# A norm and rotation phase in another order: head statistics, rotations and gate pieces of two attentions

## What is computed

```python
def mla_mixer(c_q, c_kv, k_rope, g_qa, w_uq, g_kva, w_ukv, g_qn, g_kn, cos, sin):
    q = (rmsnorm(c_q, g_qa) @ w_uq).reshape(b, s, 4, 96)
    kv = (rmsnorm(c_kv, g_kva) @ w_ukv).reshape(b, s, 4, 128)
    k_nope, v = split(kv, [64])                 # k = [k_nope, k_rope]
    q = rmsnorm(q, g_qn); k = rmsnorm(k, g_kn)  # over the 96 of a head
    q, k = rotated in their last 32 of 96
    return softmax(q k^T / sqrt(96)) v          # 4 heads

def diff_mixer(q_in, k_in, v_in, g_qn, g_kn, ..., g_sub):
    q = apply_rope(rmsnorm(q_in.reshape(b, s, 8, 32), g_qn))
    k = apply_rope(rmsnorm(k_in.reshape(b, s, 8, 32), g_kn))
    o = (softmax(q1 k1^T) - lam * softmax(q2 k2^T)) v      # 4 heads
    return rmsnorm(o, g_sub) * (1 - lambda_init)

merged = sum over the branches n (mla, fnet, diff, hgrn) of
         sigmoid(gate_logits_n) * (o_n @ w_branch[n])
x = x + merged @ w_out; then a feed-forward part
```

## Time and profile before

| | us |
|---|---|
| median of three runs | 3875.69 (3874.26 to 3875.77) |
| the profiled execution | 3875.1 |
| its span, first to last instruction | 3873.0 |
| PE busy | 3719.0 (96%) |
| VectorE busy | 1826.0 (47%) |
| ScalarE busy | 1360.0 (35%) |
| GpSimd busy | 255.7 (7%) |
| mean granted clock of TensorE | 0.983 of full |

### The profile page before, as it was taken

One profiled execution on the slowest core, in us unless ns is written; L12 is line 12 of the kernel. 1 busy time (PEld: TensorE's weight loads), 2 busy tenths in 40 slices (PEclk: granted clock), 3 DMA queues, 4 the chain that ended last, 5 costly groups with the idle time before them and its releaser, 6 DMA issues.

```text
span 3873.0 us, 44934 instructions
## 1 busy us (share of the span) xinstructions
PE 3719.0 (96%) x16592; PEld 2902.9 (75%) x16592; DVE 1826.0 (47%) x2405; ACT 1360.0 (35%) x2102; POOL 255.7 (7%) x154
## 2 busy tenths in 40 slices
PE   6999699999999999999999999999999999999999
PEld 5888478887887777888756677878875666787887
DVE  7743677424333555333354657443333555654332
ACT  3222332223323554232343434332234344433321
POOL 2000200000000000000010101200000010120000
PEclk8999899999999999999999999999999999999999
DMA  7843268433332221333312122333341122232332
GB/s 268 266 135 95 84 213 268 146 100 88 97 96 85 60 64 58 102 94 95 114 47 56 50 69 58 93 92 94 95 118 49 49 59 61 63 90 88 97 94 86
DMA packets 639945, 390.83 MB, mean 101 GB/s; under 512 B 17856, under 2 KB 601408, under 8 KB 638656
## 3 DMA queue, kind: packets, MB, share of 16 engines
q1 hardware_dynamic: 634432, 376.82, 32.9%
q10 hardware_dynamic: 5376, 12.14, 0.9%
HBM read 386.81 MB, written 2.10 MB: 100 GB/s over the span
## 4 chain that ended last, share of the span: by engine, by line
PE 90%; DVE 5%; issue 2%; ACT 1%; POOL 1%; DMA 0%; ACTq 0%; DVEq 0%; POOLq 0%
PE bank L1969 25%; PE bank L1971 24%; PE bank L1970 24%; PE bank L2150 2%; PE bank L2109 1%; PE bank L1984 1%; PE bank L1985 1%; PE bank L1986 1%; PE bank L2142 1%; PE bank L2252 1%; POOL ssum L716 1%; PE bank L2294 1%; PE bank L1995 1%; PE bank L2090 1%; PE bank L2133 1%
## 5 line engine op out<-in xcount | busy, mean ns | idle before, releaser
L1296 DVE TENSOR_TENSOR w_lo<-stage,w_hi 128x1024 fp32r<-128x1024 f32 x564 | 695.7, 1234 | 1432.9 <-ACT w_hi L779 1432.3
L1969 PE MATMUL bank<-h_hi,w_hi 128*128 128x512 f32 x3008 | 1199.9, 399 | 36.9 <-DVE h_lo L1543 27.0
L1971 PE MATMUL bank<-h_hi,w_lo 128*128 128x512 f32 x3008 | 1175.6, 391 | 0.0
L1970 PE MATMUL bank<-h_lo,w_hi 128*128 128x512 f32 x3008 | 1175.4, 391 | 0.0
L779 ACT ACTIVATE w_hi<-stage 128x1024 fp32r<-128x1024 f32 x564 | 596.7, 1058 | 1224.9 <-PE bank L1971 1212.9
L1969 PEld LDWEIGHTS bank<-h_hi,w_hi 128*128 128x128 f32 x3008 | 568.0, 189 | 176.5 <-DVE h_lo L1543 29.4
L1970 PEld LDWEIGHTS bank<-h_lo,w_hi 128*128 128x128 f32 x3008 | 568.0, 189 | 122.2 <-issue 8.0
L1971 PEld LDWEIGHTS bank<-h_hi,w_lo 128*128 128x128 f32 x3008 | 567.1, 189 | 120.3
L1971 PE MATMUL bank<-a_hi,w_lo 128*128 128x512 f32 x1056 | 410.9, 389 | 0.0
L1969 PE MATMUL bank<-a_hi,w_hi 128*128 128x512 f32 x1056 | 410.9, 389 | 0.0
L1970 PE MATMUL bank<-a_lo,w_hi 128*128 128x512 f32 x1056 | 410.9, 389 | 0.0
(11 more groups left out here) (259 smaller groups left out, 3693.9 us busy)
## 6 DMA issues: line engine op xcount, KB each, us to landing
stage<-in_ffn_w_in SPq DMA_DIRECT2D x176, 512.0 KB, 3.8
stage<-in_w_in SPq DMA_DIRECT2D x108, 512.0 KB, 3.8
stage<-in_w_gate_up SPq DMA_DIRECT2D x88, 512.0 KB, 3.7
ada_stage<-in_ada_w SPq DMA_DIRECT2D x128, 256.0 KB, 3.9
work<-in_ada_w SPq DMA_DIRECT2D x128, 256.0 KB, 5.5
stage<-in_ffn_w_out SPq DMA_DIRECT2D x64, 512.0 KB, 3.5
stage<-in_w_down SPq DMA_DIRECT2D x32, 512.0 KB, 3.7
stage<-in_ffn_w_out SPq DMA_DIRECT2D x32, 384.0 KB, 3.1
```

The lines of the kernel that those rows point to most:

```text
L1296: nc.vector.tensor_tensor(lo, stage[:, slot * WORDS:(slot + 1) * WORDS], hi.bitcast(F32), ALU.subtract).then_inc(w_lo_ready, 1)
L1969: nc.tensor.matmul(dst, wh, chunk(hi, k), start=first and a == 0, stop=False)
L1970: nc.tensor.matmul(dst, wh, chunk(lo, k), start=False, stop=False)
L1971: ins = nc.tensor.matmul(dst, wl, chunk(hi, k), start=False, stop=last and a == len(ks) - 1)
```

## The change

Nothing is computed otherwise; instructions of every engine's list change places.

- MLA: PE lays the statistics in pairs: two, a quarter of gate 1, two, the value parts, two, a quarter of gate 1, two, the other half of gate 1. VectorE squares the query heads when the query parts are out and normalises four while the others are under way; ScalarE makes the roots in two groups around the value copies.
- MLA, rotations: PE does rotations 0 to 3, branch 1, gate 2, rotations 4 to 7, branch 2, fill 3. VectorE does its part of fill 1 behind the first four rotations, of fill 2 behind the other four.
- Diff: the roots of the two query chunks stand on ScalarE ahead of the sixth projection's copy. VectorE rotates all four chunks ahead of fill 8; PE does gate 8, rotations, branch 8, fills 9 and 10.
- GpSimd does the diff cosines ahead of merge 8, not behind it.
- Diff's attention with `tail=True`: gate 15 is laid into the last head (three of eight steps ahead of its transposes, five behind), and branch 15 behind it; the first hgrn projection follows, then the statistics of the result.

The diff, with the surroundings cut (in the order of the file: GpSimd, ScalarE, VectorE, PE):

```diff
...
             cosines(mla_ropes)
-            merge(step[1], DIFF_FILL)
             pool.wait_ge(rope_loaded, 32 * (step[1] + 1))
             cosines(diff_ropes)
-            for f in range(DIFF_FILL + 1, MERGES):
+            for f in range(DIFF_FILL, MERGES):
                 merge(step[1], f)
...
 
-    def attention(at_, fills):
+    def attention(at_, fills, tail=False):
         heads = at_["heads"]
...
                 output_high(h)
-            if not last:
+            if not last or tail:
                 fill(fills + h + 1)
...
         parts([wk(MLA_K + h)[0:64] for h in range(4)])
+        roots(mla_head_norms(l)[0:4])
         parts([token_rows(MLA_V, t) for t in range(TB)])
-        roots(mla_head_norms(l))
+        roots(mla_head_norms(l)[4:8])
         fill(MLA_FILL + 1)
...
         n.zbase = n.z
-        for c in range(6):
+        for c in range(5):
             project("diff", c, wk(c))
+        roots(diff_norms(l)[0:2])
+        project("diff", 5, wk(5))
         branch_high(DIFF_FILL)
         parts([token_rows(DIFF_V, t) for t in range(TB)])
-        roots(diff_norms(l))
+        roots(diff_norms(l)[2:4])
         fill(DIFF_FILL)
-        split_roped(diff_ropes, 0, 3)
+        split_roped(diff_ropes, 0, 4)
         fill(DIFF_FILL + 1)
-        split_roped(diff_ropes, 3, 4)
         fill(DIFF_FILL + 2)
-        attention(diff_attention(), DIFF_FILL + 3)
+        attention(diff_attention(), DIFF_FILL + 3, tail=True)
         roots(diff_sub_norms)
-        fill(DIFF_FILL + 7)
+
+        n.zbase = n.z
+        project("hgrn", H_ORDER[0], wk(H_ORDER[0]), func=ACT.Sigmoid)
         act.wait_ge(gnormed, n.item)
         splits([wk(DIFF_O + c) for c in range(2)], 2)
-
-        n.zbase = n.z
-        for c in H_ORDER[:6]:
+        for c in H_ORDER[1:6]:
             project("hgrn", c, wk(c), func=ACT.Sigmoid)
...
 
-    def attention(at_, fills):
+    def attention(at_, fills, tail=False):
         heads = at_["heads"]
...
         output_low(len(heads) - 1)
+        if tail:
+            fill(fills + len(heads))
         n.block += TB * mp * len(heads)
...
         fill(MLA_FILL)
+        heads = mla_head_norms(l)
+        dve.wait_ge(z_ready, n.z + 4)
+        squares(heads[0:4])
+        dve.wait_ge(z_ready, n.z + 8)
+        dve.wait_ge(kr_placed, l + 1)
+        squares(heads[4:6])
+        normalise(heads[0:4])
+        squares(heads[6:8])
+        normalise(heads[4:8])
         n.z += 12
-        dve.wait_ge(z_ready, n.z - TB)
-        dve.wait_ge(kr_placed, l + 1)
-        heads = mla_head_norms(l)
-        squares(heads)
-        normalise(heads)
-        fill(MLA_FILL + 1)
         dve.wait_ge(gnormed, n.item)
...
         ropes(mla_ropes, 0, 4)
+        fill(MLA_FILL + 1)
+        ropes(mla_ropes, 4, 8)
         fill(MLA_FILL + 2)
-        ropes(mla_ropes, 4, 8)
         fill(MLA_FILL + 3)
...
         normalise(norms)
-        fill(DIFF_FILL)
         dve.wait_ge(gnormed, n.item)
         dve.wait_ge(rope_loaded, 32 * (l + 1))
-        ropes(diff_ropes, 0, 3)
+        ropes(diff_ropes, 0, 4)
+        fill(DIFF_FILL)
         fill(DIFF_FILL + 1)
-        ropes(diff_ropes, 3, 4)
         fill(DIFF_FILL + 2)
-        attention(diff_attention(), DIFF_FILL + 3)
+        attention(diff_attention(), DIFF_FILL + 3, tail=True)
         dve.wait_ge(o_ready, n.opair)
...
         normalise(diff_sub_norms)
-        fill(DIFF_FILL + 7)
+        next_weights("hgrn", H_ORDER[0])
         splits([wk(DIFF_O + c) for c in range(2)], 2)
 
-        for c in H_ORDER[:4]:
+        for c in H_ORDER[1:4]:
             next_weights("hgrn", c)
...
 
-    def attention(at_, l, fills):
+    def attention(at_, l, fills, tail=False):
 
...
             last = h + 1 == len(heads)
+            filled = not last or tail
             if not last:
                 scores(h + 1, first)
-                if cut:
-                    gate(fills + h + 1, 0, cut)
+            if filled and cut:
+                gate(fills + h + 1, 0, cut)
             pe.wait_ge(p_scaled, (n.head + h + 1) * TB)
...
             turn(h, 1)
+            if filled:
+                gate(fills + h + 1, cut, DC)
             if not last:
-                gate(fills + h + 1, cut, DC)
                 scores(h + 1, middle)
...
             weigh(h, TB - 1)
-            if not last:
+            if filled:
                 branch(l, fills + h + 1)
...
                                             stop=True))
+        heads = mla_head_norms(l)
+        stats(heads[0:2])
+        gate(MLA_FILL + 1, 0, 2)
+        stats(heads[2:4])
         w_v = w_ukv.rearrange("p (h c) -> p h c", h=4)[:, :, 64:P]
...
                                             stop=True))
-        stats(mla_head_norms(l))
-        fill(l, MLA_FILL + 1)
+        stats(heads[4:6])
+        gate(MLA_FILL + 1, 2, 4)
+        stats(heads[6:8])
+        gate(MLA_FILL + 1, 4, DC)
         pe.wait_ge(z_ready, n.z)
+        pe.wait_ge(gnormed, n.item - 4)
+        ropes(mla_ropes, 0, 4)
+        branch(l, MLA_FILL + 1)
+        gate(MLA_FILL + 2)
         pe.wait_ge(gnormed, n.item)
-        ropes(mla_ropes, 0, 4)
-        fill(l, MLA_FILL + 2)
         ropes(mla_ropes, 4, 8)
+        branch(l, MLA_FILL + 2)
         fill(l, MLA_FILL + 3)
...
         stats(norms[2:4])
-        fill(l, DIFF_FILL)
+        gate(DIFF_FILL)
         pe.wait_ge(z_ready, n.z)
...
         ropes(diff_ropes, 0, 4)
+        branch(l, DIFF_FILL)
         fill(l, DIFF_FILL + 1)
...
         pe.wait_ge(qk_ready, n.qk)
-        attention(diff_attention(), l, DIFF_FILL + 3)
-        gate(DIFF_FILL + 7, 0, 4)
+        attention(diff_attention(), l, DIFF_FILL + 3, tail=True)
+
+        n.zbase = n.z
+        project("hgrn", H_ORDER[0])
         stats(diff_sub_norms)
-        gate(DIFF_FILL + 7, 4, DC)
-        branch(l, DIFF_FILL + 7)
-
-        n.zbase = n.z
-        for c in H_ORDER:
+        for c in H_ORDER[1:]:
             project("hgrn", c)
...
```

## The result

The changed kernel takes **3850.4 us** (median of four runs, 3848.2 to 3853.4), the kernel before 3875.7 (3874.3 to 3877.6): ratio 0.9934, interval 0.9920 to 0.9949. It is faster by 25.3 us, where 21.7 were forecast; 3854.0 (3844 to 3868) was the prediction.

The account below looks back on a forecast made before the run. PE bounds the kernel, losing time to idling and low clock in three stretches per layer. MLA 13.4, diff 0.5 and last head 7.3 sum to 21.2 off 3875.1: 3853.9, the median 0.6 above, so 3854 (3844 to 3868).

Parts of the forecast that it names:

- MLA, statistics: MLA's statistics, spread between gate quarters and value parts, cost PE zero idle, so it reaches the rotations at 2002.2.
- MLA, rotations: With fills behind each four rotations on VectorE, MLA's scores start 5.2 us earlier in one layer, 3.9 in layer 1.
- The rival with fills in the quiet: GpSimd's later cosines leave fill 1 and the last low halves alone: 8 us faster, 3846; chance 0.13.
- The scores' clock: MLA's first scores run at the high clock level after a short last wait: 2.3 us more, 2.0 in layer 1.
- Diff, rotations: In differential attention, a new 5.5 us wait at branch 9 replaces waits of 3.34 and 2.0: 0.5 us gained in all.
- Last head: At diff's last head, gate 15 matmuls fill idle before the transposes and statistics follow the first hgrn projection: 7.3 us.
- The rule on ACT_TABLE_LOAD: A ScalarE table switch costs a 1.38 us drain besides its load, delaying the third projection: gain 2.8 us less.
- The slower rival: GpSimd's cosines hold VectorE for all their time in the MLA and diff chains: 3880; chance 0.05.

Follow-up runs that it names:

- diff_fill_inside: The changed kernel with VectorE's fill 8 in the differential attention between its first two and last two rotations, ScalarE's splits divided to match: 3839.2 us.
- mla_only: The kernel before with only the MLA part of the change (statistics, fills, root groups): 3860.2 us.
- mla_early_ropes: The changed kernel with PE's first four MLA rotations ahead of gate 1's last piece, and ScalarE's first query split ahead of gate 1's tanh: 3862.5 us.
- diff_norm_only: The kernel before with only the differential attention's norm and rotation changed (roots in two groups, fill 8 behind all four rotations): 3873.8 us.
- tail_only: The kernel before with only the differential attention's last head changed (gate matmuls inside it, statistics behind the next part's first projection): 3867.4 us.
- short_cosines: The changed kernel with GpSimd's cosine product on 16 of the 512 columns, nearly all of it left out: 3828.8 us.

## Why the prediction was right

**MLA, statistics: right.** Zero idle was assumed between them, and the trace has none. The rotations start at 2001.49 (2002.2 forecast).

**MLA, rotations: right, 1 us too small a layer.** The scores gained 6.2 and 4.8 us by layer (5.2 and 3.9). Of the steps, VectorE reached fill 1 at 2014.68 instead of 2016.0; fill 1 took 4.14 (4.19), four rotations 8.24 (7.88), fill 2 2.15 (2.30). The missed microsecond is the way to fill 1: PE 0.7 us earlier, and GpSimd took 6.0 us for four cosines where I had used the older 6.9. Branch 2 waited 3.7 (4.3 forecast). Branch 3 waited 0.65 and not 1 to 3, since the slow clock behind branch 2 took most of PE's room. The rival with fills in the quiet falls by the 4.14 of fill 1. The scores' clock gave 2.3 and 1.8 us (2.3 and 2.0).

**Diff, rotations: right.** The new wait is 5.12 us (5.5), the slow clock behind it 2.4 us; 0.8 and 1.0 us gained (0.4 and 0.1). The prediction named its cause, fill 8 behind all four rotations; diff_fill_inside confirms it by taking it away, for 11.2 us. That the gain itself came out at 1.8 us where 0.5 was forecast says little: mla_only won 1.7 in the same stretch without this edit.

**Last head: right.** 3.9 + 3.3 = 7.2 us (7.3). The sum has a slip that did no harm: PE's busy time in layer 1 was read as 16.8 where the row says 16.51, so 14.9 and not 15.1 stands beside the 14.8 taken. And the idle time of 3.5 us ahead of these transposes did not bring the low level at the same point each time: in layer 1 of the kernel before they took 1.09 us behind 3.50, and only the matmuls behind them were slow; in layer 0 they took 1.97 behind 3.51.

**The rule on ACT_TABLE_LOAD** of the Trainium skill (page "ScalarE: Activation LUTs", section "What ACT_TABLE_LOAD costs") would have made this 2.8 us less. The runs don't bear it out: the third projection waited 0.54 us in both layers, as forecast without it, and in the rows of mla_early_ropes above, the load of 1.28 us starts 0.02 us behind the activation's end and the tanh 0.01 behind the load's. No drain shows.

**The slower rival: the mechanism is there, at a smaller size.** It had VectorE held for all of GpSimd's time, and 3880. In the early_ropes rows four operations of 0.70 us take 6.7, beside four cosines that take 6.4 (mla_early_ropes): the two engines take turns. This is what the Trainium skill, page "SBUF — State Buffer", section "SBUF: two separate sides", states of VectorE operations with two SBUF inputs: whichever engine starts first keeps the shared ports for its whole instruction. These rows agree with it. GpSimd is held too: the shortest of these four cosines takes 1.27 us, the median 1.73.

```profile
L723 POOL TENSOR_TENSOR work<-work,extra x4: 1273/1729/1736, 2001.5 to 2006.1; 96x512 f32<-96x512 f32 x4
```

The rival's mistake is that it took all of GpSimd's time as VectorE's loss. In rotations and fills a part of VectorE's operations read PSUM, and those go on (0.68 us beside a cosine as without one); and GpSimd's 13.2 us hold some 3 of its own waiting (eight products of 1.27 are 10.2, an estimate). So 6.3 us are lost, not 13.2.

**What no step had.** The steps as measured add up to 24.1 us: in MLA 6.2 + 4.8 + 2.3 + 1.8, diff 1.8, last head 7.2. Taken between the same matmuls, as in the table of the parts, they are 23.6: MLA 15.0, diff 1.8, last head 6.8. The profiled spans differ by 25.9 (3873.0 - 3847.1). The other 2.3 lie in one place, which the change doesn't touch: the 48 matmuls behind the norm of layer 1, 13.8 us before, 11.5 after. So what the forecast of 21.2 stands against are 23.6 us, 1.6 of the difference in MLA and 1.3 in diff, with 0.5 the other way in the last head; the last 2.3 of the measured gain came from a place that it didn't have, and can't be counted for the change.

```profile
2876.12 0.47 PE L1990 MATMUL bank<-h_hi,w_hi 128*128 128x512 f32 x1 [3.38 <-DVE h_lo L1344]
```

PE is idle for 3.40 us ahead of them before and 3.38 after. Over 14 profiled kernels (before, after, the twelve of the experiments) that idle time is 3.31 to 3.56 us, and the 48 matmuls take 11.4 to 11.5, 12.6 or 13.8 to 13.9, in no order with it: diff_norm_only has 11.44 behind 3.31, mla_only 13.81 behind 3.31. With the edits there may be an order: the three that take 13.8 (before, mla_only, tail_only) are the three without diff's part. One profile of each can't tell that from chance. The ten runs of diff_norm_only reach from 3869.8 to 3875.2 us, and its profile is the fastest of them. So up to 2.3 us of any difference between two profiled runs here can be this.

## To carry to other kernels

When PE waits for another engine's chain, first ask whether that chain is late by its length or by its order: moving one item within it adds no work and shows which (11 us in one attention, no clear gain in the other). If it is late by its length, let the idle time stand in the middle of the phase, where the slow clock behind it is covered, and not ahead of the last step (3.9 us over both layers here). Work given to GpSimd isn't free for VectorE: count the VectorE operations with both inputs in SBUF that lie beside it, at up to 1.1 us each here.

## What the runs showed that I had not expected

- GpSimd beside VectorE: 0.70 us becomes up to 1.8 for an operation with both inputs in SBUF, 0.68 stays 0.68 for one that reads PSUM.
- The clock behind an idle time: after 3.7 us of waiting at branch 2 the next 30 matmuls took 2.8 us more; after 5.1 us at branch 9 the loss was 2.4 and 2.0; after 1.1 us (diff_fill_inside) next to nothing. The length of the wait alone doesn't tell the price. After 3.3 to 3.6 us behind the layer-1 norm it was nothing, 1.1 or 2.3 us from kernel to kernel, with the same code there. And a shorter wait isn't safe: in short_cosines branch 9 waits 2.04 us in both layers, and its stretch behind the wait had a granted clock of 0.67 (1.7 us lost) in layer 0 and of 1.00 in layer 1. Why one or the other comes isn't settled by these runs.
- Plain f32 matmuls of 128 x 512, put in to keep the clock, took 0.89 us each, where the split ones take 0.23.
